# Early modulation tiles loaded in halves, and column sums of the modulation made by transposes and VectorE reductions

## What is computed

```python
def adaln(cond, w, b):                       # w is 2048 x 6144
    m = jax.nn.silu(cond) @ w + b
    return jnp.split(m, 3, axis=-1)          # shift, scale, gate: 2048 each

# layer i:
shift, scale, gate = adaln(c, ada_w[i], ada_b[i])
h = modulate(rms_norm(x, norm_g[i]), shift[:, None], scale[:, None])
shift_c, scale_c, gate_c = adaln(c_ctx, ada_w[i], ada_b[i])      # layer 0 only
hc = modulate(rms_norm(ctx, norm_g[i]), shift_c, scale_c)
...
x = x + gate[:, None] * y
```

## Time and profile before

| | us |
|---|---|
| median of 3 runs | 2675.39 (2670.93 to 2676.15) |
| the profiled execution, its own time | 2676.03 |
| its span (first to last instruction) | 2674.3 |
| PE busy | 2630.7 (98%) |
| DVE busy | 1708.4 (64%) |
| ACT busy | 476.1 (18%) |

### The profile page before, as it was taken

How to read it: one execution, slowest core, us unless ns; L and a number is a source line. 1 busy time by engine, 2 the same in 40 slices (tenths; PEclk the granted TensorE clock), 3 DMA queues, 4 the chain that set the end, 5 groups by cost and what they waited for, 6 DMA issues and landing times. The chain is left out here.

```text
span 2674.3 us, 45594 instructions
## 1 busy us (share of the span) xinstructions
PE 2630.7 (98%) x19157; PEld 2382.2 (89%) x19157; DVE 1708.4 (64%) x2953; ACT 476.1 (18%) x930; POOL 61.1 (2%) x85
## 2 busy tenths in 40 slices
PE   5999999999999999999999999999999999999999
PEld 1399999999997877777778999999999999999999
DVE  6677767777685666666655536656666655556643
ACT  2121212121111222222220002111111111122211
POOL 1000000000000000000000000000000000000000
PEclk9899999999999999999999999999999999999999
DMA  9955755576556233333354455555545454555542
GB/s 378 326 176 191 246 185 182 183 237 205 162 175 193 82 114 114 114 114 114 114 204 155 145 174 170 177 158 170 175 157 176 143 166 152 155 159 162 164 144 77
DMA packets 382154, 453.84 MB, mean 170 GB/s; under 512 B 20804, under 2 KB 352184, under 8 KB 380984
## 3 DMA queue, kind: packets, MB, share of 16 engines
q1 hardware_dynamic: 350096, 352.03, 42.2%
q0 software_dynamic: 21776, 83.89, 8.7%
q10 hardware_dynamic: 10136, 15.79, 1.6%
HBM read 443.49 MB, written 8.19 MB: 169 GB/s over the span
## 5 line engine op out<-in xcount | busy, mean ns | idle before, releaser
L631 PE MATMUL bank<-hT,w 128*128 128x128 f32 (+2 forms) x6240 | 898.3, 302 | 4.7 <-ACT hT L1368 3.1
L631 PEld LDWEIGHTS bank<-hT,w 128*128 128x128 f32 x6240 | 785.8, 193 | 103.4 <-issue 88.2
L631 PE MATMUL bank<-yT,w 128*128 128x128 f32 (+1 forms) x3776 | 526.3, 299 | 1.0 <-DVE yT L2331 1.0
L631 PEld LDWEIGHTS bank<-yT,w 128*128 128x128 f32 x3776 | 493.2, 192 | 22.8 <-DVE yT L2331 1.2
L1368 ACT ACTIVATE work<-bank 128x512 f32<-128x512 f32 (+3 forms) x294 | 151.5, 522 | 1228.0 <-PE bank L631 1143.8
L631 PE MATMUL bank<-hT,work 128*128 128x128 f32 x2672 | 316.8, 275 | 0.0
L631 PEld LDWEIGHTS bank<-hT,work 128*128 128x128 f32 x2672 | 307.5, 192 | 0.0
L631 PEld LDWEIGHTS bank<-w,hT 128*128 128x128 f32 x1792 | 245.0, 191 | 19.3 <-issue 5.7
L631 PE MATMUL bank<-w,hT 128*128 128x128 f32 (+2 forms) x1792 | 261.3, 305 | 0.0
L1368 ACT ACTIVATE work<-work 128x512 f32<-128x512 f32 (+3 forms) x299 | 168.6, 570 | 272.6 <-DVE work L2181 155.0
L2024 DVE SCALAR_TENSOR_TENSOR work<-xT,silc,work 128x512 f32<-128x512 f32 x240 | 180.3, 751 | 37.5 <-DMA xT<-in_ada_w 30.6
(11 more groups left out here) (235 smaller groups left out, 2404.3 us busy)
## 6 DMA issues: line engine op xcount, KB each, us to landing
w<-in_na_ssd_w_in SPq DMA_DIRECT2D x47, 2048.0 KB, 11.1
xT<-in_ada_w POOLq DMA_DIRECT2D x64, 1024.0 KB, 8.4
w<-in_sc_w_in SPq DMA_DIRECT2D x32, 2048.0 KB, 9.2
w<-in_w_in SPq DMA_DIRECT2D x32, 2048.0 KB, 9.4
w<-in_na_ssd_w_out SPq DMA_DIRECT2D x16, 2048.0 KB, 9.8
w<-in_na_ssd_w_in SPq DMA_DIRECT2D x18, 1024.0 KB, 8.8
w<-in_sc_w_out SPq DMA_DIRECT2D x8, 2048.0 KB, 8.4
w<-in_w_out SPq DMA_DIRECT2D x8, 2048.0 KB, 8.6
```

The source lines that it names most:

```text
L631: return nc.tensor.matmul(dst, lhsT, rhs, start=start, stop=stop, skip_group_check=free)
```

## The change

Four edits, made together.

1. PE's early tiles 1 to 5 are loaded in two halves of 1 MB as well, each half with a semaphore of its own per slot (`early_half[s]`, then `w_loaded[s]`), and `early_tile` waits for the first half, does two slabs, and then waits for the second. Tile 6 remains one load.
2. `early_turn` makes its eight columns with 2-row transposes instead of matmuls.
3. `early_sums(b)` becomes `early_sums(b, k)`, k for c or c_ctx: PE transposes the eight 128x128 pieces of an accumulator into two whole banks (`EARLY_BANKS[k]`: banks 1 and 3, or 4 and 5), and DVE adds up along the free dimension with two reductions of 128 x (4 x 128) to 4 (`early_added_up`). For b = 3 this stands on DVE between `early_part(6)` and `early_part(7)`, and waits for PE's tile 5; for b = 2 one half stands ahead of `first_norm(0)`, the other behind it. The bias is added in an instruction of its own.
4. `late_sums` becomes `late_turned`: eight transposes into banks 3 and 4, and `late_mod` does two such reductions and then the bias. The wait for `na_lnfree` is gone with bank 2.

Semaphores are merged to make room (`x_saved` and `x_back` into `x_moved`, `q_half` into `early_half[0]`), and `one_zero` with its two memsets goes.

```diff
@@ SP
+            s = EARLY_SLOT[t]
+            if t < 6:
+                sp.dma_start(early(s)[:, 0:2, :], early_columns(b, q, (0, 1))).then_inc(early_half[s], 16)
+                sp.dma_start(early(s)[:, 2:4, :], early_columns(b, q, (2, 3))).then_inc(w_loaded[s], 16)
             else:
-                sp.dma_start(early(EARLY_SLOT[t]), early_columns(b, q)).then_inc(w_loaded[EARLY_SLOT[t]], 16)
+                sp.dma_start(early(s), early_columns(b, q)).then_inc(w_loaded[s], 16)
@@ PE
-                if t in (0, 7) and kc == 2:
+                if kc == 2 and t != 6:
                     pe.wait_ge(w_loaded[s], 16 * (1 + EARLY_SLOT[:t].count(s)))
...
-                last = mm(early_place(b, ch), row, IDENT[0:2, 0:2], n == 0 and ch == 0, n == 1 and ch == 7, True)
+                last = tr(early_place(b, ch), row, 2)
...
-        def early_sums(b):
+        def early_sums(b, k):
             for ch in range(8):
-                for k in range(2):
-                    last = mm(early_place(b, ch), eaccs[b][:, k, ch * P:(ch + 1) * P], one_zero[:, 2 * k:2 * k + 2],
-                              b == 3 and ch + k == 0, b == 2 and ch + k == 8, True)
+                last = tr(EARLY_BANKS[k][ch // 4][:, (ch % 4) * P:(ch % 4 + 1) * P], eaccs[b][:, k, ch * P:(ch + 1) * P])
...
         pe.wait_ge(early_taken, 4)
-        early_sums(3)
+        pe.wait_ge(xt_act, DC)
+        for k in range(2):
+            early_sums(3, k)
...
         pe.wait_ge(early_taken, 8)
-        early_sums(2).then_inc(ada_used, 1)
+        early_sums(2, 0).then_inc(ada_used, 1)
+        early_sums(2, 1)
         early_turn(1, 1).then_inc(ada_used, 1)
...
-        def late_sums(a, norms):
+        def late_turned(a):
             pe.wait_ge(late_taken, 8 * a + 8)
-            pe.wait_ge(na_lnfree, norms)
             for block in range(2):
                 for ch in range(4):
-                    n = 8 * block + 2 * ch
-                    last = mm(bank[2][:, n:n + 2], aacc[:, block, ch * P:(ch + 1) * P], ONES[:, 0:2])
+                    last = tr(bank[3 + block][:, ch * P:(ch + 1) * P], aacc[:, block, ch * P:(ch + 1) * P])
@@ DVE
-        for t in range(5, 8):
-            early_part(t)
+        early_part(5)
+        early_part(6)
+        def early_added_up(b, k):
+            for half in range(2):
+                at = 8 * b + 4 * half
+                last = v.tensor_reduce(mod[:, 0, at:at + 4, k:k + 1].rearrange("p a b -> p (a b)"),
+                                       EARLY_BANKS[k][half][:, :].rearrange("p (a b) -> p a b", a=4), AX.X, ALU.add)
+            return last
+        dve.wait_ge(ada_used, 6)
+        early_added_up(3, 0)
+        early_added_up(3, 1)
+        early_part(7)
...
-        link(v.tensor_tensor(mod[:, 0, 16:32, :], bank[3][:, 0:32].rearrange("p (a b) -> p a b", b=2), bias[:, 16:32, :],
-                             ALU.add))
+        link(early_added_up(2, 0))
+        link(v.tensor_tensor(mod[:, 0, 16:32, 0:1], mod[:, 0, 16:32, 0:1], bias[:, 16:32, 0:1], ALU.add))
         amplitude(0, 0, 0)
...
         first_norm(0, range(3, DC))
+        link(early_added_up(2, 1))
+        link(v.tensor_tensor(mod[:, 0, 16:32, 1:2], mod[:, 0, 16:32, 1:2], bias[:, 16:32, 1:2], ALU.add))
         amplitude(1, 0, 1)
...
-            v.tensor_tensor(mods[:, ds(at, 8), 0:1], bank[2][:, 0:16].rearrange("p (a b) -> p a b", b=2)[:, :, 0:1],
-                            colp[:, ds(at, 8)].unsqueeze(2), ALU.add).then_inc(mod_ready, 1)
+            for block in range(2):
+                last = v.tensor_reduce(mods[:, ds(at + 4 * block, 4), 0:1].rearrange("p a b -> p (a b)"),
+                                       bank[3 + block][:, :].rearrange("p (a b) -> p a b", a=4), AX.X, ALU.add)
+            link(last)
+            v.tensor_tensor(mods[:, ds(at, 8), 0:1], mods[:, ds(at, 8), 0:1], colp[:, ds(at, 8)].unsqueeze(2),
+                            ALU.add).then_inc(mod_ready, 1)
```

More of the change, by code:

```diff
@@ L179, in chunk @@
         return t[:, ds(c, 1), :].rearrange("p a b -> p (a b)")
+    EARLY_BANKS = ((bank[1], bank[3]), (bank[4], bank[5]))
     def both_diagonals(ap):
@@ L191, in program @@
     eaccs = {2: L(2, 4 * TILE), 3: L(2, 4 * TILE)}
-    crow, squares_of_rows, one_zero = L(P), L(4), L(4)
+    crow, squares_of_rows = L(P), L(4)
     L = Lay(work, WORK)
@@ L402, in program @@
     w_loaded = [sem(f"w_loaded{s}") for s in range(SLOTS)]
-    ada_used, ada_row, q_half = sem("ada_used"), sem("ada_row"), sem("q_half")
-    early_half, early_v = sem("early_half"), [sem(f"early_v{p}") for p in range(3)]
+    ada_used, ada_row = sem("ada_used"), sem("ada_row")
+    early_half, early_v = [sem(f"early_half{s}") for s in range(3)], [sem(f"early_v{p}") for p in range(3)]
     late_in = [sem(f"late_in{r}") for r in range(2)]
-    early_taken, late_taken, late_sum, x_saved, x_back, y_saved, y_back, wdt_in = (sem(n) for n in ("early_taken", "late_taken", "late_sum", "x_saved", "x_back", "y_saved", "y_back", "wdt_in"))
+    early_taken, late_taken, late_sum, x_moved, y_saved, y_back, wdt_in = (sem(n) for n in ("early_taken", "late_taken", "late_sum", "x_moved", "y_saved", "y_back", "wdt_in"))
     consts_in, params_zeroed, c_in, params_in, x_in, ctx_in, ssd_in = (
@@ L469, in _ @@
                         "p a (b c) -> p (a b) c", c=T)).then_inc(early_v[place], 16)
-        gp.wait_ge(x_saved, 16)
+        gp.wait_ge(x_moved, 16)
         gp.wait_ge(norm_mul, DC)
@@ L509, in _ @@
         b, q = EARLY_PE[7]
-        sp.dma_start(early(1)[:, 0:2, :], early_columns(b, q, (0, 1))).then_inc(early_half, 16)
+        sp.dma_start(early(1)[:, 0:2, :], early_columns(b, q, (0, 1))).then_inc(early_half[1], 16)
         sp.dma_start(early(1)[:, 2:4, :], early_columns(b, q, (2, 3))).then_inc(w_loaded[1], 16)
@@ L548, in _ @@
                 sp.wait_ge(xt_act, EIGHT)
-                sp.dma_start(x_scratch, xT[:, :, :].rearrange("p a b -> p (a b)")).then_inc(x_saved, 16)
+                sp.dma_start(x_scratch, xT[:, :, :].rearrange("p a b -> p (a b)")).then_inc(x_moved, 16)
             if n % 4 == 1 and n > 4:
@@ L583, in out_proj @@
                 if is_first(i) and s == 1:
-                    sp.dma_start(xT[:, :, :].rearrange("p a b -> p (a b)"), x_scratch).then_inc(x_back, 16)
+                    sp.dma_start(xT[:, :, :].rearrange("p a b -> p (a b)"), x_scratch).then_inc(x_moved, 16)
                 if is_first(i) and s == 2:
@@ L702, in early_tile @@
             s = EARLY_SLOT[t]
-            if t in (0, 7):
-                pe.wait_ge(early_half, 16 if t == 0 else 32)
+            if t == 6:
+                pe.wait_ge(w_loaded[s], 16)
             else:
-                pe.wait_ge(w_loaded[s], 16 * (1 + EARLY_SLOT[:t].count(s)))
+                pe.wait_ge(early_half[s], 16 * (1 + EARLY_SLOT[:t].count(s)))
             tile = w[s][:, :, :].rearrange("p a b -> p (a b)").rearrange("p (a b) -> p a b", a=4)
             for kc in range(4):
-                if t in (0, 7) and kc == 2:
+                if kc == 2 and t != 6:
                     pe.wait_ge(w_loaded[s], 16 * (1 + EARLY_SLOT[:t].count(s)))
@@ L816, in na_unit @@
             if n == 0:
-                pe.wait_ge(q_half, 16)
+                pe.wait_ge(early_half[0], 48)
                 featured(bank[0][:, 0:T], s, 0, T, lambda kc: kc + 1, range(EIGHT))
@@ L861, in na @@
                 na_transposes(a, 1)
-                late_sums(a, 3 * i + 1)
+                late_turned(a)
             na_unit(i, 3)
@@ L945, in ssd @@
                 na_transposes(7, 1)
-                late_sums(7, 24)
+                late_turned(7)
                 featured(dst[:, :], 0, 1, T + TC, None, range(EIGHT, DC)).then_inc(acc_full, 1)
@@ L1891, in _ @@
         v.memset(prm, 0.0).then_inc(params_zeroed, 1)
-        link(v.memset(one_zero, 0.0))
-        link(v.memset(one_zero[:, 0:4:3], 1.0))
         dve.wait_ge(cols_pe, 1)
@@ L2500, in _ @@
         token_sums(OUT_IN[1], OUT_SUM[1], (0, EIGHT), link)
-        dve.wait_ge(x_back, 16)
+        dve.wait_ge(x_moved, 32)
         add_out()
```

5 lines of the change are left out of this document (1 added, 4 removed).

## The result

The changed kernel takes 2658.96 us (median of 4 runs, 2656.67 to 2659.24), the kernel before, run beside it, 2675.49 (4 runs, 2670.93 to 2676.15). The ratio is 0.9942, with a 95% interval of 0.9931 to 0.9954. The prediction was 2659, range 2653 to 2667. The profiled execution took 2658.91 us, its span is 2657.2.

The account below looks back on a forecast made before the run. PE, busy 98% of the span, was taken as the bound, with load waits and a backlog early. Gains of 8.6 + 1.4 + 6.8 = 16.8 us from 2676.03 gave 2659.2, stated as 2659 us; range 2653 to 2667.

Parts of the forecast that it names:

- 8.6: Early stage up to PE's second sums: they begin at 110.7 in place of 119.28, 8.6 us earlier.
- 1.4: Tail from the second sums into the first projection: 5.8 us in place of 7.2, a gain of 1.4 us.
- 6.8: Late sums: PE saves 0.85 us in each of eight places by transposes, 6.8 us.
- Late sums and their cover: Late sums: 6.8 us saved on PE; DVE's added reductions fit in its 4.39 us of idle time, costing nothing.
- Halves: Early tiles: landings stay, half of PE's work precedes each second half; tile 1 ends at 41.4, tile 3 at 71 to 72.5.
- halves don't help: Rival, early stage: PE keeps its dates up to 77.1, only shorter turn and sums win 3.8 us; 2664, chance 0.11.
- its two reasons: Why halves might not help: both halves land together, or the clock takes back what the earlier starts give.
- The clock: Early stage: sums as transposes not expected to pull the clock down; first projection left as is, 2 us either way.
- The rival in which the clock falls in the mixer: First mixer: clock falls behind sixteen transposes, 3.4 us in each of eight places, 27 us more; 2686, chance 0.03.
- the step: DVE in the early stage: four reductions ahead of part 7 cost 2.8 us, 2.2 idle before; part 7 ends at 110.0.

## Why the prediction was right, and where it was not

**The sum.** 8.6 + 1.4 + 6.8. The first two, 10.0, measured 10.2 to the projection's start (8.2 up to the second sums, 1.9 behind, against 8.6 and 1.4); the third measured 6.9 behind it. The dates on the way came out too: tile 3 at 71.7 (71 to 72.5), tile 6 the one that waits, tile 7 at 111.0 (109 to 111.5), part 7 ending at 110.1 (110.0), projection at 116.28 (116.5), 0.88 in place of 1.71 (0.87).

**Late sums and their cover.** Right in size and reason. The kernel with these alone shows the 7 us, and doubling the reductions shows that DVE's idle time covers them.

**Halves.** The time was right, the cause wrong: that the 8.6 came out is luck. The prediction carried the earlier end of tiles 1 to 3 through to tile 7 and counted it in the 8.6. It did see that tile 6 would catch PE, and did not ask what PE's date there would be without the halves. The kernel with the sums alone and the kernel without the halves answer: the same, 116.1 to 116.4. Either way PE comes to wait: with halves for tile 6, until 94.36, without them for DVE's part 7, until 110.86. What brings PE to tile 7 in time are the sums and the turn. The prediction gave their shorter instructions 3.8 us ("halves don't help", 2664, with a chance of 0.11, was worked out from these alone). It left out that tiles 4 to 6 then run at full speed: 9.95 and 16.53 become 7.03 and 13.9, another 5.6 us.

These 5.6 are counted against the execution that it started from; against the one with the projection at 120.76, whose tiles 4 to 6 had the full clock with the old sums, the kernel without halves starts the projection 4.7 us earlier, near the 3.8 and 1.4 that the rival has for the instructions. So the rival's outcome was met, that halves win nothing, and against the execution of the prediction its price lacked what the clock gives back. Of its two reasons one is refuted (the halves landed apart: PE did the first half of tile 3 from 62.95 on, and the second from 68.06); the other holds in part (behind the wait for tile 6 that tile took 8.73 in place of 7.03).

**The clock.** The direction was right: 64 transposes in a row don't pull it down, 64 instructions of two columns do; the long sums in the mixer show both. In the early stage the 32 of the first sums were followed by a low clock in four of the five profiles that have them. The size was left out of the sum, and against the profiled execution it is more than half of the early gain (5.6 of 10.2). The rival in which the clock falls in the mixer is refuted by 64 transposes in a row.

**DVE.** Part 7 ended at 110.1 as forecast, but through its load: DVE was idle until 100.07 on the DMA, 0.65 us later than before, against the sum, which kept this load's landing where it was. The reductions, 686 ns each (0.69 was taken), were done at 99.2, so what the step counted as their price was the load's.

**The execution it started from.** The 10 us of early gain hold against the profiled execution of 2676.03. The two profiles in which the same early stage found the clock higher start the projection at 120.16 and 120.76, so against these the early gain is 3.9 and 4.5 us. The kernel before has runs down to 2668.9, and in the three comparisons on one chip each the changed kernel's median is 16.5, 12.2 and 13.9 us below that of the kernel before. The time itself came out because the changed kernel's own dates were built up from the landings of PE's tiles, which stay within 0.8 us of the old ones, and mostly at the full clock, which it then had.

## What to carry to other kernels

When an engine waits for loads that stand in a queue, find the last place where the data catch it, and price an earlier start by what is left of it there; what stands ahead of that place is handed back. A sum over partitions by float32 matmuls of two columns is two instructions on TensorE, each with a weight load, and rows of 32 or 64 of these could let its clock fall for the work behind them, while rows of 16 in the mixer did not. A transpose is one such instruction and kept the clock; it costs half of that (0.88 in place of 1.71 us for eight), if VectorE has the idle time for the reduction. And take the spread of the kernel before into account before trusting one profile of a stage in which TensorE pauses: the clock there differs from run to run.

## What the runs showed of the hardware that was not expected

- The same early stage took 126.45 and 120.16 us in two executions with PE waiting for its tiles to the same dates within 0.3 us; the rows differ in which tiles ran at 1.2 GHz. A third took 120.76 with tile 3 starting 0.85 us later than in the first. Runs of the kernel before spread over 7.7 us on one chip, those of the changed kernel over 3.9 in three comparisons, those of the two kernels with PE's idle time filled over 1.1 and 1.4, those of the unfilled kernel without halves over 1.7. That the spread is the clock's fits the mean granted clock of the runs; no run varied the clock alone.
- A 2-row transpose of 128 columns takes 0.08 us in a row of eight (0.65 us), where the matmul of the same size took 0.24 (1.94 us for eight, two instructions each, at PEclk 1.00 in the kernel with the halves alone and in that with the late sums alone; the 2.35 of the kernel before was at a lower clock); the prediction had 1.2 us for the eight.
- POOL's last early load does not keep its date as PE's tiles do: DVE starts part 7 behind it at 99.42 in the kernel before, at 100.07 to 100.49 in the changed kernel, and at 102.11 in the kernel with only the late sums. SP's loads go with it: in the two profiles of the kernel before SP issued tile 7's loads at 90.5 us, and the last of POOL's four pieces landed 12.8 and 12.9 us after its issue; in the changed kernel and in that with only the late sums SP issued them at 80.4 to 86.1, and it took 13.9 to 15.3. That they delay it fits this, and was not tried by itself.
